# Diagonal 32x32 score blocks of the recurrent pairs made in the projection phase, and inverted on GpSimd in the recurrent phase straight from memory

## The chip, the cores and the metric
One core of a Trainium2 chip runs the whole kernel. The metric is the device time of one execution in microseconds. Engines: TensorE (PE, its weight loads PEld), VectorE (DVE), ScalarE (ACT), GpSimd (POOL) and SyncE (SP), which here issues nearly all DMAs, in program order on one queue.

## The reference, cut to what matters
Two layers over 1024 latent and 256 context tokens, batch 1. The change touches the RWKV-7 half of layer 0: eight heads of 64, forward and backward.

```python
def rwkv7_scan(r, w, k, v, a, bvec, state):
    xs = tuple(jnp.moveaxis(t.astype(jnp.float32), 2, 0) for t in (r, w, k, v, a, bvec))

    def step(s, inp):
        r_t, w_t, k_t, v_t, a_t, b_t = inp
        sa = jnp.einsum('bhvk,bhk->bhv', s, a_t)
        s = s * w_t[:, :, None, :] + sa[..., None] * b_t[:, :, None, :] + v_t[..., None] * k_t[:, :, None, :]
        return s, jnp.einsum('bhvk,bhk->bhv', s, r_t)
...
        return (rh, to_heads(w, RWKV_HEADS), kh, vh, -kk, kk * ah), bonus
```

The kernel does this scan in chunks of 128 tokens. The term with `sa` makes each chunk need the inverse of a triangular 128x128 matrix, the unit matrix less the strict triangle of the scores of `b` against `a`. The inverse is built from the inverses of its four diagonal 32x32 blocks.

## The kernel before, in words
All data are float32; large products are made from a high and a low part in three products. The phases run one after the other, with a barrier of all engines between them.

**Projection phase** (`project_phase`, L668). The input projection is made in 26 tiles of 128 columns (`TILES0`), each over 1280 tokens in three pieces (512, 512, 256). SyncE loads the weights two tiles ahead (L707). ScalarE evicts a tile (L911), VectorE shifts and mixes it (L479, L487), SyncE stores it (L796). Between these tiles the four pairs of heads are prepared: pair p has the five tiles from b = 5 + 5p. The table `PREP_PE` says behind which piece of which tile TensorE makes the small products of a pair, all in two PSUM banks, 6 and 7, in turn: `w0` and `a0` in tile b, `w1`, `a1` and `ksum` in tile b+1, `bonus` in tile b+5. A product waits until the last but one use of the banks is evicted. `w0` and `a0` read `wab` (`w_pair_lr`), which SyncE loads for the pair at tile b (L763). VectorE prepares the pair in steps at the head of its tiles (`prep`): step 3 ends with L995, step 4 with L1010, and step 0 of the next pair waits for `bonus` (L967). The results go to `in_d` (`put`, L751).

**Recurrent phase** (`rwkv_units`, L1044). Each pair is cut in two halves of five chunks: eight halves n. TensorE makes the scores of the five chunks (`bx`, `kx`, L1199), transposes (`nat`), `z`; then come `y32`, `d32`, `t32`, `y64`, `t64`, which build the 128x128 inverses, and `wu` and `out`, which use them. The scores of half n+1 stand ahead of the use of half n, and `y32(n)` stands at the last chunk of the scores of half n+1. The inversion goes round by memory: SyncE waits for the scores of half n in `N`, stores their diagonal blocks to `blk_d` in eight DMAs (L1110), and loads them again with one block to a partition, the forward ones to `U`, the backward ones to `Ut` (L1117). GpSimd turns the backward ones into `U` (L1561), and inverts by 30 steps of two instructions (L1566, L1568), then copies the transposes to `Ut` (L1573). SyncE stores both (L1126) and brings them back in 14 DMAs (L1122) to `XQ`, `XE` and `N`, for which `y32(n)` waits.

```python
                for n in range(HALVES):
                    if n + 1 < HALVES:
                        blocks_in(n + 1)
                    if n + 2 < HALVES:
                        for m in half_chunks(n + 2):
                            sp.wait_ge(s["out_dve"], m - NCH + 1)
                            load(m)
```

Of the kernel before, what the change touches and what calls it, by code (L numbers as in the profile page):

```python
# [55 lines left out]
def constants():  # L56
# [10 lines left out]
    c["side"] = ((p % 4) == np.arange(4)[None]).astype(one)  # L67
    c["neg"] = np.concatenate([np.where(f >= p, 0, -BIG), np.where(f <= p, 0, -BIG)], 1).astype(one)
    c["pick"] = np.concatenate([np.broadcast_to(p % 32 == 0, (P, P)), np.broadcast_to(p % 32 == 1, (P, P))], 1).astype(one)
# [7 lines left out]

    c["score"] = np.concatenate([(f > p), (f >= p), (f < p), (f <= p)], 1).astype(one)
    c["heads"] = ((p // 64) == (f // 64)).astype(one)
# [4 lines left out]
def const_layout():  # L84

    at, n = {}, 0
    for k, v in constants().items():
        at[k] = (n, n + v.shape[1])
        n += v.shape[1]
    return at, [at["parted16"][0], at["score"][0], n]  # L90
# [430 lines left out]
PREP_SEQ = [(name, p, i) for key in sorted(PREP_PE) for name, p in PREP_PE[key] for i in range(3)]  # L521
BY_ACT = [x for x in PREP_SEQ if x[0][0] in "wa"]
BY_DVE = [x for x in PREP_SEQ if x[0][0] not in "wa"]

# [143 lines left out]
def project_phase(nc, A, G, xnat, hi, lo, LW, LA):  # L668

    win = A.p["e_w_in"][0].rearrange("(k p) n -> p k n", p=P)  # L670
    with ExitStack() as ctx:
# [19 lines left out]
        mus, keep = sb("mix_mus", [P, 18, 4]), sb("mix_keep", [P, 18])  # L691
        PS = G.PS
# [20 lines left out]
        def job(n):  # L713
# [6 lines left out]
                "pp_ps by_act by_dve sq_ok c_ok ln_ok root e_ok pl_ok ready0 ready1 rk_ok kh_ok st0 st1 st_pl st_bonus pstep half_ok")  # L720
        with phase(nc, sems) as (block, s):
# [26 lines left out]
            def _(sp):  # L748
# [37 lines left out]
                sp.dma_start(G.cst_rwkv[:], A.consts[:, G.ends[1]:G.ends[2]]).then_inc(s["consts"], 16)  # L786
                for n in range(last + 1):
# [16 lines left out]
                sp.wait_ge(s["st_bonus"], 64)  # L804

            @block.tensor
            def _(pe):
                def prep_product(name, p):
                    for i in range(3):
                        x, bank = piece_of(name, p, i)  # L810
                        t, m = pieces(i)
                        if x >= 2:
# [2509 lines left out]
```

## Time and profile before

| | us |
|---|---|
| median of 3 runs | 3097.58 |
| lowest, highest | 3096.53, 3099.73 |
| the profiled execution | 3096.0 |
| its span in the trace | 3094.2 |
| TensorE busy | 2581.2 (83%) |
| VectorE busy | 1597.5 (52%) |
| ScalarE busy | 902.9 (29%) |
| GpSimd busy | 742.2 (24%) |

Times in the trace count from the span's start. The projection's tiles run from about 230 to 633 us and the recurrent phase from 640 to about 1165 us. The busy shares are means over many phases; what a change in one phase is worth has to be read there. PE slices in tenths, 40 of equal length: `6899999965688864676775999999599999998887`.

### The profile page before, as it was taken

Reading aid. Unit: us, or ns where it says so; the run is one execution under the profiler, and the core shown is the slowest. Engines: PE = TensorE matmul, PEld = TensorE weight load, DVE = VectorE, ACT = ScalarE, POOL = GpSimd, SP = SyncE. Lnnn points to the kernel's source line nnn. Section 1 sums busy time; section 2 is a strip of 40 time slices with the busy share of each in tenths; the row PEclk is TensorE's granted clock in tenths of the full one; section 3 lists DMA queues with packets and bytes.
Section 4 is the critical chain, followed back from the end, with each engine's and each line's share of the span. In section 5 each row is a group of like instructions: output and inputs, shape, how many; then the busy total and the mean of one; then the engine's idle time right before and its main releaser. Section 6 shows DMA issues by size and latency. Waiting matters only on the chain. (4 is left out here: it accounts for less than half of the span.)

```text
span 3094.2 us, 54814 instructions
## 1 busy us (share of the span) xinstructions
PE 2581.2 (83%) x23550; PEld 2185.8 (71%) x23550; DVE 1597.5 (52%) x2411; ACT 902.9 (29%) x1464; POOL 742.2 (24%) x739
## 2 busy tenths in 40 slices
PE   6899999965688864676775999999599999998887
PEld 2577677755677752555564777777499999998665
DVE  3037887542345624785466556465544646454233
ACT  2114333311132222563202232222233333332211
POOL 1111111126466541111322111111021111111421
PEclk8999999986889876677887999999799999999898
DMA  6622555532334413120461333232402222210621
GB/s 263 223 65 80 165 146 159 165 129 77 84 77 121 108 24 98 36 60 26 155 133 55 112 102 111 97 109 99 176 35 76 89 76 90 76 55 5 217 94 60
DMA packets 291551, 319.51 MB, mean 103 GB/s; under 512 B 109807, under 2 KB 235190, under 8 KB 288750
## 3 DMA queue, kind: packets, MB, share of 16 engines
q1 hardware_dynamic: 290240, 312.64, 32.1%
q8 instruction: 186, 3.05, 0.4%
q10 hardware_dynamic: 1070, 3.37, 0.3%
q14 instruction: 55, 0.45, 0.0%
HBM read 203.32 MB, written 112.56 MB: 102 GB/s over the span
## 5 line engine op out<-in xcount | busy, mean ns | idle before, releaser
L2895 PE MATMUL PS<-Q,K 128*128 128x128 f32 x2560 | 296.5, 278 | 31.1 <-DMA K<-k_d 23.6
L2895 PEld LDWEIGHTS PS<-Q,K 128*128 128x128 f32 x2560 | 293.0, 194 | 33.7 <-issue 27.6
L3016 POOL TENSOR_TENSOR weights_lo<-weights,weights_hi 128x1664 fp32r<-128x1664 f32 x32 | 121.3, 3791 | 566.3 <-ACT weights_hi L2974 566.3
L2922 PE MATMUL PS<-V_hi,weights_hi 128*128 128x258 f32 x832 | 239.1, 287 | 5.4 <-DVE H L3125 2.8
L461 PE MATMUL PS<-hT_hi,w_in_hi 128*128 128x512 f32 (+1 forms) x640 | 239.4, 374 | 0.0
L462 PE MATMUL PS<-hT_lo,w_in_hi 128*128 128x512 f32 (+1 forms) x640 | 236.3, 369 | 0.0
L2923 PE MATMUL PS<-V_lo,weights_hi 128*128 128x258 f32 x832 | 236.1, 284 | 0.0
L463 PE MATMUL PS<-hT_hi,w_in_lo 128*128 128x512 f32 (+1 forms) x640 | 236.0, 369 | 0.0
L2924 PE MATMUL PS<-V_hi,weights_lo 128*128 128x258 f32 x832 | 235.1, 283 | 0.0
L461 PE MATMUL PS<-h_hi,w_in_hi 128*128 128x512 f32 (+1 forms) x624 | 227.9, 365 | 5.3 <-PEq L112 5.3
L2396 PE MATMUL PS<-w_out_hi,y_in_hi 128*128 128x512 f32 x416 | 168.5, 405 | 71.6 <-POOL y_in_lo L2334 30.9
L462 PE MATMUL PS<-h_lo,w_in_hi 128*128 128x512 f32 (+1 forms) x624 | 224.5, 360 | 0.0
L463 PE MATMUL PS<-h_hi,w_in_lo 128*128 128x512 f32 (+1 forms) x624 | 223.9, 359 | 0.0
L2963 ACT ACTIVATE weights<-M_row,head_cols 128x128 f32<-128x128 f32 x352 | 112.2, 390 | 201.0 <-DVE diag_arg L3073 200.9
L2736 DVE SCALAR_TENSOR_TENSOR xnew<-padl,tile_cols,xnew 128x1024 f32<-128x1024 f32 x128 | 168.6, 1318 | 3.4
L2397 PE MATMUL PS<-w_out_lo,y_in_hi 128*128 128x512 f32 x416 | 167.0, 401 | 0.0
L2398 PE MATMUL PS<-w_out_hi,y_in_lo 128*128 128x512 f32 x416 | 166.6, 400 | 0.0
L2530 POOL TENSOR_TENSOR w_in_lo<-xnew,w_in_hi 128x2048 fp32r<-128x2048 f32 x15 | 69.3, 4618 | 404.1 <-ACT w_in_hi L2527 404.1
L925 POOL TENSOR_TENSOR w_in_lo<-w_in,w_in_hi 128x1024 fp32r<-128x1024 f32 x25 | 65.6, 2625 | 402.6 <-ACT w_in_hi L856 402.6
L2922 PEld LDWEIGHTS PS<-V_hi,weights_hi 128*128 128x128 f32 x832 | 157.9, 190 | 6.0 <-issue 6.0
L2923 PEld LDWEIGHTS PS<-V_lo,weights_hi 128*128 128x128 f32 x832 | 158.7, 191 | 0.0
L2924 PEld LDWEIGHTS PS<-V_hi,weights_lo 128*128 128x128 f32 x832 | 158.4, 190 | 0.0
(412 smaller groups left out, 5692.6 us busy)
## 6 DMA issues: line engine op xcount, KB each, us to landing
chunk_in<-in_d SPq DMA_DIRECT2D x40, 512.0 KB, 3.4
w_in<-in_e_w_in_dram SPq DMA_DIRECT2D x30, 512.0 KB, 5.1
xnew<-in_o_w_in_dram SPq DMA_DIRECT2D x30, 512.0 KB, 6.1
in_d<-xnat SPq DMA_DIRECT2D x20, 640.0 KB, 6.0
modw<-in_mod_w_dram SPq DMA_DIRECT2D x12, 1024.0 KB, 9.7
xnat<-in_mod_w_dram SPq DMA_DIRECT2D x8, 1536.0 KB, 7.4
v_d<-xnew SPq DMA_DIRECT2D x16, 640.0 KB, 3.0
k_d<-xc SPq DMA_DIRECT2D x16, 640.0 KB, 2.9
```

The lines of the kernel that those rows point to most:

```text
L461: pe.matmul(PS[:, bank + off // 512, 0:n], wh[:, k], hh[:, k, t], start=(k == 0), stop=False)
L462: pe.matmul(PS[:, bank + off // 512, 0:n], wh[:, k], hl[:, k, t], start=False, stop=False)
L463: last = pe.matmul(PS[:, bank + off // 512, 0:n], wl[:, k], hh[:, k, t], start=False, stop=(k == KT - 1))
L2396: pe.matmul(out, yh[:, i % YRING, t], wh[:, k, c], start=(k == 0), stop=False)
L2397: pe.matmul(out, yh[:, i % YRING, t], wl[:, k, c], start=False, stop=False)
L2398: last = pe.matmul(out, yl[:, i % YRING, t], wh[:, k, c], start=False, stop=(k == n_k - 1))
L2736: ins = dve.scalar_tensor_tensor(lat, padl[:, a:a + ROWS, b:b + GRID_W], col[tap], lat, ALU.mult, ALU.add)
L2895: last = pe.matmul(PS[:, 4 + x % 4, (j - j0) * P:(j - j0 + 1) * P], K[:, kt, j * P:(j + 1) * P], Q[:, kt, i * P:(i + 1) * P], start=(kt == ...
L2922: pe.matmul(out, wh, VH[:, j, q], start=(j == seen[0]), stop=False)
L2923: pe.matmul(out, wh, VL[:, j, q], start=False, stop=False)
L2924: last = pe.matmul(out, wl, VH[:, j, q], start=False, stop=(j == seen[-1]))
L3016: pool.tensor_tensor(WL[n % 2][:], W[:, n % 2], WH[n % 2][:].bitcast(F32), ALU.subtract).then_inc(s["w_lo"], 1)
```

## The change
The projection phase makes the diagonal blocks itself. Behind piece 1 of tile b+4 TensorE makes `blk0` (forward), behind piece 1 of tile b+5 `blk1` (backward, already transposed), each as 80 products of 64 rows and 32 columns in two bank uses. VectorE multiplies them by a triangle into `blk`: `blk0` at the end of step 4, `blk1` at the head of step 0. SyncE stores them to `blk_d` (`blocks_away`, eight DMAs each): those of `blk0` at tile b+5 ahead of the next pair's `wab`, those of `blk1` at tile b+6, the last ones ahead of the last tile's store.

In the recurrent phase the eight stores of a half, and GpSimd's first copy, are gone; both directions are loaded to `U`. The load for half n+1 stands right behind the store of the inverses of half n, and the 14 returns are a step of their own (`blocks_back`), which now waits for the scores in `N`. Constants are ordered anew: the pair's in the projection phase, the scores' at the head of the recurrent phase, `neg` and `block4` in the output phase.

```diff
+    c["tri"] = (np.arange(32)[None] > p % 32).astype(one)
...
-    PREP_PE[_b, 0], PREP_PE[_b, 1] = [("w0", _p)], [("a0", _p)]
+    PREP_PE[_b, 0], PREP_PE[_b, 1] = [("w0", _p)], [("a0", _p)] + ([("blk1", _p - 1)] if _p else [])
...
+    PREP_PE[_b + 4, 1] = [("blk0", _p)]
+PREP_PE[PREP_AT + 4 * PREP_TILES, 1] = [("blk1", 3)]
...
+                def blocks_away(p, d):
+
+                    sp.wait_ge(s["by_dve"], BY_DVE.index((f"blk{d}", p, 1)) + 1)
+                    for i in range(2):
+                        for k in range(4):
+                            sp.dma_start(A.blk_d[2 * p + i, d, 10 * k:10 * k + 10].rearrange("b s t -> s b t"),
+                                         blk[32 * k:32 * k + 32, 5 * i:5 * i + 5].rearrange("s c h t -> s (c h) t")).then_inc(s["blk_st"], 16)
+
                 def prep_io(n):
                     p, k = job(n)
                     if p is None:
                         return
+                    if k < 2 and p:
+                        blocks_away(p - 1, k)
                     if k == 0:
...
+                blocks_away(3, 1)
                 made(sp, last)
...
+                def block_product(p, d):
+
+                    ops = (aa[0], sg[0]) if d == 0 else (sg[1], kk)
+                    for h in range(2):
+                        x, bank = piece_of(f"blk{d}", p, h)
+                        bank_free(x)
+                        q = slice(64 * h, 64 * h + 64)
+                        for c in range(NCH):
+                            for k in range(4):
+                                t = slice(c * CH + 32 * k, c * CH + 32 * k + 32)
+                                ins = pe.matmul(PS[32 * k:32 * k + 32, bank, 32 * c:32 * c + 32], ops[0][q, t], ops[1][q, t],
+                                                start=True, stop=True)
+                        ins.then_inc(s["pp_ps"], 1)
...
+                            if name == "blk0":
+                                pe.wait_ge(ready[0], 4 * p + 3)
+                                block_product(p, 0)
+                            elif name == "blk1":
+                                pe.wait_ge(ready[1], 4 * p + 2)
+                                block_product(p, 1)
...
+                def blocks(p, d):
+                    if p or d:
+                        dve.wait_ge(s["blk_st"], 128 * (2 * p + d))
+                    for h in range(2):
+                        x, bank = piece_of(f"blk{d}", p, h)
+                        dve.wait_ge(s["pp_ps"], x + 1)
+                        dve.tensor_tensor(blk[:, :, h], PS[:, bank, 0:32 * NCH].rearrange("p (c t) -> p c t", t=32),
+                                          G.c("tri")[:, None, :].broadcast_to([P, NCH, 32]), ALU.mult).then_inc(s["by_dve"], 1)
...
                     if k == 0 and p:
+                        blocks(p - 1, 1)
                         dve.wait_ge(s["v_in"], 16 * p)
...
                         dve.scalar_tensor_tensor(khs, R, col(p, J_RK), khs, ALU.mult, ALU.mult).then_inc(s["rk_ok"], 1)
+                        blocks(p, 0)
...
                 def blocks_in(n):
-                    sp.wait_ge(s["bx_sb"], HC * (n + 1))
+
+                    if n:
+                        sp.wait_ge(s["zt_ok"], n)
+                        sp.wait_ge(s["zu_st"], 32 * n)
+                    else:
+                        sp.wait_ge(s["zero"], 1)
                     for d in range(2):
-                        for k in range(4):
-                            sp.dma_start(A.blk_d[n, d, 10 * k:10 * k + 10].rearrange("b s t -> s b t"),
-                                         diag(d, n, k, k).rearrange("s c h t -> s (c h) t")).then_inc(s["rel_st"], 16)
-                    sp.wait_ge(s["rel_st"], 128 * (n + 1))
-                    if n:
-                        sp.wait_ge(s["zu_st"], 32 * n)
-                        sp.wait_ge(s["zt_st"], 32 * n)
-                    for d, dst in enumerate((U, Ut)):
-                        sp.dma_start(dst[64 * d:64 * d + 40].rearrange("b s t -> b (s t)"),
+                        sp.dma_start(U[64 * d:64 * d + 40].rearrange("b s t -> b (s t)"),
                                      A.blk_d[n, d].rearrange("b s t -> b (s t)")).then_inc(s["rel_in"], 16)
...
+                sp.dma_start(G.cst_rwkv[:], A.consts[:, G.ends[3]:G.ends[4]]).then_inc(s["consts"], 16)
                 for m in half_chunks(0):
                     load(m)
+                blocks_in(0)
...
-                sp.wait_ge(s["zero"], 4)
-                blocks_in(0)
                 blocks_out(0)
+                blocks_in(1)
+                blocks_back(0)
...
-                    if n + 1 < HALVES:
-                        blocks_in(n + 1)
...
                         blocks_out(n + 1)
+                        if n + 2 < HALVES:
+                            blocks_in(n + 2)
+                        blocks_back(n + 1)
...
-                    step.link(pool.tensor_copy(U[64:104], Ut[64:104].rearrange("b s t -> b t s")))
+                    if n:
+                        pool.wait_ge(s["zt_st"], 32 * n)
```

SyncE at tile 10 of the projection, the first tile of pair 1, where `w_in` is a tile's weight load. Before:

```order
L796 DMA v_d<-p_out 128x1280 [waits mixed]
L707 DMA w_in<-in_e_w_in_dram 128x8x128 [waits lo_ok,hi_ok]
L763 DMA w_pair_lr<-in_rwkv_ww_f_dram 64x128 [waits pp_ps]
L763 DMA w_pair_lr<-in_rwkv_wa_f_dram 64x128
L763 DMA w_pair_lr<-in_rwkv_ww_b_dram 64x128
L763 DMA w_pair_lr<-in_rwkv_wa_b_dram 64x128
L766 DMA pair_bufs<-v_d 128x1280 [waits kh_ok]
```

The same place in the changed kernel:

```order
L812 DMA v_d<-p_out 128x1280 [waits mixed]
L713 DMA w_in<-in_e_w_in_dram 128x8x128 [waits lo_ok,hi_ok]
L764 DMA blk_d<-blocks_out 32x10x32 [waits by_dve]
L764 DMA blk_d<-blocks_out 32x10x32 x7
L779 DMA w_pair_lr<-in_rwkv_ww_f_dram 64x128 [waits pp_ps]
L779 DMA w_pair_lr<-in_rwkv_wa_f_dram 64x128
L779 DMA w_pair_lr<-in_rwkv_ww_b_dram 64x128
L779 DMA w_pair_lr<-in_rwkv_wa_b_dram 64x128
L782 DMA pair_bufs<-v_d 128x1280 [waits kh_ok]
```

Eight stores that wait for VectorE now stand between the weight load and the four loads of `w_pair_lr`.

SyncE in the recurrent phase, from the last chunk load of one half on. Before:

```order
L1104 DMA chunk_in<-v_d 128x128
L1126 DMA inv_d<-blocks 40x1024 [waits inv_ok]
L1126 DMA inv_d<-blocks 40x1024
L1126 DMA invt_d<-blocks_t 40x1024 [waits zt_ok]
L1126 DMA invt_d<-blocks_t 40x1024
L1122 DMA inv_first<-inv_d 32x10x32 [waits zu_st,y64_ps]
...
L1122 DMA chunk_scores<-invt_d 32x10x32 x4
L1110 DMA blk_d<-chunk_scores 32x10x32 [waits bx_sb]
L1110 DMA blk_d<-chunk_scores 32x10x32 x7
L1117 DMA blocks<-blk_d 40x1024 [waits zt_st,zu_st,rel_st]
L1117 DMA blocks_t<-blk_d 40x1024
L1103 DMA chunk_in<-in_d 128x1024 [waits out_dve]
```

The same place in the changed kernel:

```order
L1159 DMA chunk_in<-v_d 128x128
L1175 DMA inv_d<-blocks 40x1024 [waits inv_ok]
L1175 DMA inv_d<-blocks 40x1024
L1175 DMA invt_d<-blocks_t 40x1024 [waits zt_ok]
L1175 DMA invt_d<-blocks_t 40x1024
L1169 DMA blocks<-blk_d 40x1024 [waits zu_st,zt_ok]
L1169 DMA blocks<-blk_d 40x1024
L1185 DMA inv_first<-inv_d 32x10x32 [waits zu_st,y64_ps,bx_sb]
...
L1185 DMA chunk_scores<-invt_d 32x10x32 x4
L1158 DMA chunk_in<-in_d 128x1024 [waits out_dve]
```

The load of the next half's blocks has moved ahead of the returns, and the stores between are gone.

## Rows read from the trace of the kernel before

**Rows 1.** The list of waits, whole span: engine, line, waited for, total, times, longest.

```profile
PE PS L1259 <- DMA chunk_scores<-invt_d: 88.5, 8, 39.0
```

**Rows 2.** TensorE's timeline: start, us, line, operation, in brackets idle time and its releaser.

```profile
724.79 0.26 PE L1259 MATMUL PS<-inv_first,chunk_scores 32*32 32x32 f32 x1 [39.03 <-DMA chunk_scores<-invt_d]
...
786.10 0.26 PE L1259 MATMUL PS<-inv_first,chunk_scores 32*32 32x32 f32 x1 [12.40 <-DMA chunk_scores<-invt_d]
...
1139.19 0.26 PE L1259 MATMUL PS<-inv_first,chunk_scores 32*32 32x32 f32 x1 [21.70 <-DMA chunk_scores<-invt_d]
```

**Rows 3.** GpSimd's timeline, the first inversion.

```profile
675.63 1.99 POOL L1561 COPY blocks<-blocks_t 40x1024 f32<-40x1024 f32 x1 [31.65 <-DMA blocks_t<-blk_d]
677.68 0.16 POOL L1562 MEMSET blocks<- 104x32 f32 x1
...
713.04 1.91 POOL L1573 COPY blocks_t<-blocks 104x1024 f32<-104x1024 f32 x1
```

**Rows 4.** SyncE's timeline of DMA issues in the recurrent phase.

```profile
646.05 0.44 SPq L1104 DMA_DIRECT2D chunk_in<-v_d  x1
...
665.18 3.87 SPq L1110 DMA_DIRECT2D blk_d<-chunk_scores  x8
671.77 0.34 SPq L1117 DMA_DIRECT2D blocks<-blk_d  x1
...
713.01 0.65 SPq L1126 DMA_DIRECT2D inv_d<-blocks  x2
...
757.20 0.32 SPq L1103 DMA_DIRECT2D chunk_in<-in_d  x1
...
784.68 5.25 SPq L1110 DMA_DIRECT2D blk_d<-chunk_scores  x8
...
1058.20 1.35 SPq L1150 DMA_DIRECT2D sG_in<-g_d  x1
```

**Rows 5.** TensorE's timeline, small products and what follows them.

```profile
726.01 1.11 PE L1226 MATMUL PS<-cst,chunk_in 128*128 128x128 f32 x4
...
743.68 0.28 PE L1345 MATMUL PS<-chunk_in,wu 128*64 128x64 f32 x4
743.79 0.29 PE L1348 MATMUL PS<-wu,chunk_in 128*64 128x64 f32 x4
...
852.60 2.08 PE L1298 MATMUL PS<-inv_first,chunk_scores 64*64 64x64 f32 x34 [0.39 <-DVE inv_first L1610]
```

**Rows 6.** VectorE's timeline in the projection phase, and ScalarE's eviction of tile 9.

```profile
318.44 3.69 DVE L993 SCALAR_TENSOR_TENSOR xnat<-pair_bufs,xnat 128x1280 f32<-128x1280 f32 x1
344.01 1.55 DVE L1010 SCALAR_TENSOR_TENSOR pair_bufs<-pair_bufs,vc 128x1280 f32<-128x1280 f32 x1
...
440.91 1.55 DVE L1010 SCALAR_TENSOR_TENSOR pair_bufs<-pair_bufs,vc 128x1280 f32<-128x1280 f32 x1
...
530.12 1.55 DVE L1010 SCALAR_TENSOR_TENSOR pair_bufs<-pair_bufs,vc 128x1280 f32<-128x1280 f32 x1
...
328.67 1.24 ACT L911 ACTIVATE xnat<-PS 128x1280 f32<-128x1280 f32 x1 [11.59 <-PE PS L463]
```

**Rows 7.** SyncE's timeline, first and last of the four loads of pair 1.

```profile
331.37 1.16 SPq L763 DMA_DIRECT2D w_pair_lr<-in_rwkv_ww_f_dram  x1
...
333.86 0.60 SPq L763 DMA_DIRECT2D w_pair_lr<-in_rwkv_wa_b_dram  x1
```

**Rows 8.** TensorE's timeline, `w0` of pairs 1, 2 and 3.

```profile
336.86 3.67 PE L821 MATMUL PS<-LW,w_pair_lr 64*128 64x512 f32 x4 [2.77 <-DMA w_pair_lr<-in_rwkv_wa_b_dram]
...
435.93 3.75 PE L821 MATMUL PS<-LW,w_pair_lr 64*128 64x512 f32 x4 [5.02 <-DMA w_pair_lr<-in_rwkv_wa_b_dram]
...
530.95 3.21 PE L821 MATMUL PS<-LW,w_pair_lr 64*128 64x512 f32 x4 [3.80 <-DMA w_pair_lr<-in_rwkv_wa_b_dram]
```

**Rows 9.** Groups of instructions by line, 350 to 1100 us: count, busy us, mean ns, idle before.

```profile
L1604 DVE COPY chunk_in<-PS 128x256 f32<-128x256 f32 x40 | 16.8, 420 | 98.1 <-PE PS L1239 98.1
```

**Rows 10.** Busy us by stretch: PE, PEld, DVE, ACT, POOL; then PEclk, DMA share, GB/s.

```profile
337.00:347.00 10.00, 9.59 (x18) 5.27 (x19) 9.82 (x9) 3.02 (x4) 0.00 (x0) 0.50 0.66 183
```

More of the change, by code:

```diff
@@ L89, in const_layout @@
         n += v.shape[1]
-    return at, [at["parted16"][0], at["score"][0], n]
+    return at, [at["neg"][0], at["parted16"][0], at["heads"][0], at["score"][0], n]
 class Names:
@@ L804, in _, with bank_free @@
                 sp.wait_ge(s["st_bonus"], 64)
+                sp.wait_ge(s["blk_st"], 16 * 16 * 4)
             @block.tensor
             def _(pe):
+                def bank_free(x):
+                    if x >= 2:
+                        before = PREP_SEQ[x - 2]
+                        if before in BY_ACT:
+                            pe.wait_ge(s["by_act"], BY_ACT.index(before) + 1)
+                        else:
+                            pe.wait_ge(s["by_dve"], BY_DVE.index(before) + 1)
+                def block_product(p, d):
[10 more added lines that the diff above has]
+                        ins.then_inc(s["pp_ps"], 1)
                 def prep_product(name, p):
@@ L971, in prep @@
                             dve.wait_ge(st[1], 64 * p)
+                            dve.wait_ge(s["pp_ps"], PREP_SEQ.index(("blk1", p - 1, 1)) + 1)
                             dve.wait_ge(s["st_bonus"], 16 * p)
@@ L1055, in rwkv_units @@
         AR = [sb(f"key_scores{i}", [P, 2, 2, 2, P]) for i in range(2)]
+        G.cst_rwkv = sb("cst_rwkv", [P, G.ends[4] - G.ends[3]])
         U, Ut, tmp = sb("blocks", [P, 32, 32]), sb("blocks_t", [P, 32, 32]), sb("block_tmp", [P, 256])
@@ L1067, in rwkv_units @@
         loads = " ".join(f"ld{c}" for c in range(NCH))
-        sems = (loads + " once zero bx_ps bx_sb kx_ps kx_sb rk_sb nat_ps nat_sb z_ps z_sb rel_st rel_in inv_ok zt_ok zu_st zt_st x_in y32_ps y32_sb "
+        sems = (loads + " consts once zero bx_ps bx_sb kx_ps kx_sb rk_sb nat_ps nat_sb z_ps z_sb rel_in inv_ok zt_ok zu_st zt_st x_in y32_ps y32_sb "
                 "d32_ps d32_sb t32_ps t32_sb y64_ps y64_sb t64_ps t64_dve t64_act wu_ps wu_sb out_ps out_dve out_act "
@@ L1132, in blocks_out, with blocks_back, back @@
                     away(Ut, A.invt_d, s["zt_st"])
+                def blocks_back(n):
+                    def back(dst, src, k):
+                        sp.dma_start(dst, src[10 * k:10 * k + 10].rearrange("b s t -> s b t")).then_inc(s["x_in"], 16)
+                    sp.wait_ge(s["bx_sb"], HC * (n + 1))
                     if n:
                         sp.wait_ge(s["y64_ps"], n)
+                    else:
+                        sp.wait_ge(s["zero"], 4)
                     sp.wait_ge(s["zu_st"], 32 * (n + 1))
@@ L3234, in const @@
             if b <= ends[1]:
-                return G.cst0[:, a - ends[0]:b - ends[0]]
-            return G.cst_rwkv[:, a - ends[1]:b - ends[1]]
+                return G.cst_late[:, a - ends[0]:b - ends[0]]
+            if b <= ends[2]:
+                return G.cst0[:, a - ends[1]:b - ends[1]]
+            if b <= ends[3]:
+                return G.cst_pair[:, a - ends[2]:b - ends[2]]
+            return G.cst_rwkv[:, a - ends[3]:b - ends[3]]
         G.c = const
@@ L3253, in build @@
             gla_units(nc, A, G)
+        B = Names()
+        G.cst_late = sb("cst_late", [P, G.ends[1] - G.ends[0]])
+        B.gates = sb("gates1", [P, LRT])
         with ExitStack() as c1:
@@ L3264, in maps_in @@
                         eng.dma_start(B.wg[:, :, a, j], A.p[n][0][a * INNER:(a + 1) * INNER].rearrange("(t p) h -> p t h", p=P)).then_inc(sem, 16)
-                return 16
+                eng.dma_start(G.cst_late[:], A.consts[:, G.ends[0]:G.ends[1]]).then_inc(sem, 16)
+                return 17
             xnew = c1.enter_context(nc.sbuf_tensor("xnew", [P, NCH, D], F32))
```

33 lines of the change are left out of this document (14 added, 19 removed).

## The prediction
> **What bounds the kernel now.** I read four views in this order. The page's first table and its slices say that TensorE is busy 83% of the span, and that its busy share is down to 0.4 to 0.8 in slices 9 to 16, where the recurrent phase of the RWKV pairs lies. The list of waits then names what TensorE waits for there: the block inverses that come back from memory [rows 1]. 88.5 us of matmul idle time stand there, in eight waits, one for each half pair. The PE timeline shows the size of single ones [rows 2]: 39.03 us before the first `y32` product, 12.40 before the second, 21.70 before the last. The other 15.4 us are five short waits between. The other rows tell why. GpSimd starts the first inversion at 675.63 [rows 3], when SyncE has stored the blocks (L1110 from 665.18) and loaded them again (L1117 from 671.77) [rows 4], and both follow the scores of the half. From the last GpSimd product of an inversion to `y32` it takes 724.79 - 713.01 = 11.8 us [rows 2, 4]. So one half costs GpSimd a copy, 35.4 us of products [rows 3], and then the round trip. The way from the end of one inversion to the start of the next goes through two trips to memory, and TensorE waits for it.
>
> **Recurrent phase, what goes.** The eight block stores leave this phase, and the load for half n+1 stands right behind the store of the inverses of half n. GpSimd's period becomes 35.4 + 0.2 + 2.0 (the copy to `blocks_t`) + some 5 for store and load, about 43 us. TensorE's ready points for the first two waits are 685.8 and 773.7, and its stage from 724.79 to 773.7 takes 48.9 us. So GpSimd is no longer the bound.
> First half: SyncE issues the load of `blocks` after the last load of half 0 [rows 4], at 646.05 + 0.44, plus 0.45 for the constants that now stand ahead: 646.9. Issue to GpSimd's start took 675.63 - 671.77 = 3.9 us on a quiet queue; behind 2.9 MB of chunk loads I add 2.2 (my estimate, from 0 to 5): 653.0. Memset and products end at 688.6. With 11.8 for the way back and 0.7 for the next load, now ahead of it, `y32` starts at 701.1. TensorE is ready at 685.8 + 0.9, the 0.9 being the constants' load in front. So 14.4 of the 39.03 us stay.
> Halves 1 to 6: the return now starts when the chunk loads of the next half are issued, since the inverse is ready by then. Last load at 757.20 + 0.8, then 11.8 us less the copy of 2.0 plus the load of 0.7: 10.5, so 768.5 against a ready point of 773.7 [rows 2, 4]. 5 us of cover are left; if the loads in flight take it, the wait is back.
> Last half: the extra loads end at 1059.55; store of the inverses and load of the next blocks take 6.4, inversion 35.6, return 11.8: 1113.4 against a ready point of 1117.5. Covered by 4 us.
> Sum: 88.5 - 14.4 - 0.9 = **73.2 us saved**. TensorE's clock adds a little: in the stage after a wait it is at half speed. After the large waits at 786 and before 1139 some of that goes; I take 3 us (bounds 0 and 15). **-76 us.**
>
> **Projection phase, what comes.** Each pair gets two products of 80 matmuls of 64 rows and 32 columns, four evictions on VectorE, and 16 stores.
> *Matmuls.* No such shape is in the trace. The nearest is `y32`, whose 40 matmuls of 32x32 took 726.01 - 724.79 = 1.22 us at half clock, 30 ns each. In `out`, two products of 64 columns in two column halves of the same rows start 0.11 us before the next pair, 55 ns each. The upper bound is `y64`: 34 records, two to a matmul, in 2.08 us, 122 ns [rows 5]. I take 30 ns, the row of the same width: 2.4 us for 80 (bounds 1.6 and 9.8). The Trainium skill (TensorE: Matmul & The Clock Gate, Part 3) says that weight loads overlap running matmuls only where the row group differs; here four matmuls in turn share it. By that rule the 80 would run one by one; the two column halves in [rows 5] speak against it. Of eight products, `blk1` of all four pairs and the last `blk0` lie on TensorE's path: 5 x 2.4 = **12 us**. `blk0` of pairs 0 to 2 is hidden in the stall that comes next. It waits for VectorE's L993, done at 322.1 in pair 0 [rows 6], and TensorE reaches it when the last piece of tile 9 is due, some 3 us before that tile's eviction at 328.67 [rows 6], so it adds no wait of its own.
> *The new wait.* This is the term that matters. VectorE masks `blk0` at the end of its step 4, behind L1010. TensorE is one tile ahead of it: it wants `w0` of the next pair after piece 0 of the next tile. Two things now tie `w0` to VectorE. Its bank is the one that `blk0` used. And SyncE waits for the masked blocks, issues eight stores, and only then loads `w_pair_lr`, which `w0` reads. Before, that load was issued from 331.37 to 334.46 and `w0` ran at 336.86 [rows 7, 8]. Now: L1010 ends at 345.56 [rows 6]; two evictions of 320 columns at 0.53 each (scaled from 0.42 for 256 columns [rows 9]): 346.6; eight stores at 4.6 (3.87 and 5.25 were seen [rows 4]): 351.2; four loads 3.1, landing 2.4: 356.7. That is 19.9 us after 336.86. The same 11.2 us after L1010 give 453.6 against 435.93, 17.7 us, and 542.9 against 530.95, 12.0 us. These add up, since VectorE's work from tile b+2 to L1010 is one unbroken row that starts from an eviction of TensorE's tile: **49.6 us**. The clock costs nothing more: TensorE fell to 0.50 of full clock (1.2 GHz) after its 2.77 us of idle already [rows 8, 10].
> *End of the phase.* The last eight stores stand ahead of the last tile's store: **4.6 us**. The other evictions, 0.5 us each, lie in VectorE's wait for `bonus`. The stores of `blk1` lie in SyncE's idle time in the next tile.
> Together **+66 us**.
>
> **Rest.** The front load is 0.2 MB smaller, the same bytes come back in the output phase as a seventeenth load beside others: 0.
> Sum: -76 + 66 = **-10 us**. The profiled execution took 3096.0 us, so 3086; it lies 1.6 below the median of the three runs, which is inside their spread. A difference of 0.2% (6 us) is about what a measurement here can tell.
>
> **Rivals.**
> 1. *Slower: the returns queue behind chunk loads.* In halves 1 to 6 the 14 returns and the load of blocks are now issued within a microsecond of 2.9 MB of loads. For it: in [rows 4] they used to run alone. Against: 5 us of cover, and odd stages are longer. It decides from a delay of 5 us; at 10 us each, six halves give 30 back: 3116. Chance 0.13.
> 2. *Slower: the block products run one by one*, 9.8 us each, 5 x 7.4 = 37 more: 3123. For it, the rule named above and `y64`'s row; against, the column halves in `out`. By the skill's rule the time would come out here. Chance 0.12.
> 3. *The clock comes back with the waits.* If the use stages after the second, fourth, sixth and last half ran at full clock throughout, some 5 us each are won, 20 in all: 3066. For it, the half clock after waits; against, those stages have short waits of their own. Chance 0.13.
> 4. *The new wait is not there*, because `w0` is served from elsewhere or VectorE is earlier than in [rows 6]: 3036. I see no way in the code. Chance 0.04.
> The forecast itself has 0.58.
>
> **How the numbers follow.** 3086 with +-12 for the forecast's own bounds: stores at 3.87 or 5.25 move it by 3, the matmul pace between 20 and 55 ns by 10, the first half's load by 3. The range reaches to rival 3 below and to 3120 above, so that most of rival 1 is in and most of rival 2 out: 3060 to 3120. Faster by over 0.2%: 0.36 of the forecast's 0.58, and rivals 3 and 4: 0.53. Within 0.2%: 0.17 of the forecast and 0.02 of rival 1: 0.19. Slower: the rest, 0.28.
>
> **What would show it.** In the profile after: `y32` waits once, some 14 us, at the first half, and hardly after; GpSimd's first inversion starts some 22 us earlier in its phase than at 675.63, and each next one runs while TensorE uses the half before. In the projection phase TensorE's waits for `w_pair_lr` grow from 2.8, 5.0 and 3.8 us to about 23, 23 and 16. The first `y32` start lies some 42 us later than 724.79, since 66 us have come and 24 have gone by then. It is wrong if the three `w0` waits stay under 10 us, if a block product takes over 4 us, or if `y32` waits in the middle halves.

## The result, and the profile after

| | before | changed |
|---|---|---|
| median, us | 3098.55 | 3078.57 |
| lowest, highest, us | 3096.53, 3099.73 | 3075.57, 3090.57 |
| runs | 4 | 4 |
| the profiled execution, us | 3096.0 | 3090.57 |
| its mean granted clock | 0.899 | 0.904 |

The ratio is 0.9943, with a 95% interval from 0.9916 to 0.9971: faster by 9 to 26 us, best estimate 18. The forecast was 10 us, so the sign is right, and the time lies 7 us below the forecast and inside the range.

The two profiled executions differ by 5.4 us only, since the profile of the changed kernel is its slowest of four executions. All sums below are made between profiles, part by part; the 12 us between this profile and its median come back at the end. Among the executions of the experiments three fell out by far (3253.58, 6453.2 and 13092.65 us); medians and ratios leave these slow ones out.

First the list of waits of the changed kernel; L1319 answers to [rows 1]. Columns: engine, line waited at, releaser, total us, times, longest.

```profile
POOL blocks L1623 <- DMA blocks<-blk_d: 109.0, 8, 19.0
...
PE PS L856 <- DMA w_pair_lr<-in_rwkv_wa_b_dram: 44.8, 3, 19.7
...
PE PS L1319 <- DMA chunk_scores<-invt_d: 25.4, 4, 19.3
...
PE PS L844 <- issue: 5.6, 2, 3.2
...
PE PS L463 <- issue: 3.0, 2, 1.5
```

The wait for the block inverses fell from 88.5 us to 25.4. GpSimd still waits 109.0 us for blocks: it is now ahead of TensorE, and after the first half `y32` waits for inverses only 6.1 us in all. The wait of `w0` for `w_pair_lr` rose from 11.6 us, the sum of the three in [rows 8], to 44.8. Two lines are new and have no releaser at all: `issue`, on the block products (L844) and on the large product right behind them (L463), 8.6 us together.

TensorE's timeline, the `y32` products that waited; they answer to [rows 2]:

```profile
773.26 0.26 PE L1319 MATMUL PS<-inv_first,chunk_scores 32*32 32x32 f32 x1 [19.30 <-DMA chunk_scores<-invt_d]
...
821.92 0.21 PE L1319 MATMUL PS<-inv_first,chunk_scores 32*32 32x32 f32 x1 [1.14 <-DMA chunk_scores<-invt_d]
...
1092.87 0.21 PE L1319 MATMUL PS<-inv_first,chunk_scores 32*32 32x32 f32 x1 [1.53 <-DMA chunk_scores<-invt_d]
...
1133.32 0.26 PE L1319 MATMUL PS<-inv_first,chunk_scores 32*32 32x32 f32 x1 [3.41 <-DMA chunk_scores<-invt_d]
```

Only the first half still waits long. Where the phases begin and end is best read on SyncE: its first issue in the recurrent phase, and its first load of the phase after. Before the change:

```profile
640.52 0.32 SPq L1103 DMA_DIRECT2D chunk_in<-in_d  x1
...
1214.52 1.13 SPq L1795 DMA_DIRECT2D gla_nat<-gq_d  x2
```

and in the changed kernel, with the last stores of the projection phase and the load of the first blocks:

```profile
696.21 5.62 SPq L764 DMA_DIRECT2D blk_d<-blocks_out  x8
701.89 0.45 SPq L815 DMA_DIRECT2D gg_d<-p_out  x1
708.06 0.36 SPq L1220 DMA_DIRECT2D cst_rwkv<-in_consts_dram  x1
...
714.95 1.05 SPq L1169 DMA_DIRECT2D blocks<-blk_d  x2
...
1208.60 1.15 SPq L1857 DMA_DIRECT2D gla_nat<-gq_d  x2
```

The recurrent phase starts 708.06 - 640.52 = **67.5 us later**, and lasts 1208.60 - 708.06 = 500.5 us where it lasted 574.0, **73.5 us less**. What follows takes the same time (1879.7 and 1880.2 us to the end of the span). That is the whole account: +67.5 - 73.5 + 0.5.

**The 67.5 us.** TensorE's timeline at the first block product and the `w0` behind it:

```profile
328.20 1.53 PE L844 MATMUL PS<-xnat 64*32 64x32 f32 x154
...
332.96 0.33 PE L844 MATMUL PS<-xnat 64*32 64x32 f32 x6 [3.23 <-issue]
...
356.72 3.77 PE L856 MATMUL PS<-LW,w_pair_lr 64*128 64x512 f32 x4 [13.60 <-DMA w_pair_lr<-in_rwkv_wa_b_dram]
```

`w0` of pair 1 starts at 356.72 instead of 336.86 [rows 8], 19.9 us later. Those of pairs 2 and 3 follow:

```profile
475.53 3.78 PE L856 MATMUL PS<-LW,w_pair_lr 64*128 64x512 f32 x4 [19.75 <-DMA w_pair_lr<-in_rwkv_wa_b_dram]
...
581.95 3.78 PE L856 MATMUL PS<-LW,w_pair_lr 64*128 64x512 f32 x4 [11.50 <-DMA w_pair_lr<-in_rwkv_wa_b_dram]
```

against 435.93 and 530.95, so 39.6 and 51.0 us late. The chain behind it stands on VectorE and SyncE. VectorE:

```profile
346.55 1.55 DVE L1063 SCALAR_TENSOR_TENSOR pair_bufs<-pair_bufs,vc 128x1280 f32<-128x1280 f32 x1
348.01 0.88 DVE L1005 TENSOR_TENSOR blocks_out<-PS,cst_pair 128x320 f32<-128x320 f32 x2
```

SyncE:

```profile
348.92 3.86 SPq L764 DMA_DIRECT2D blk_d<-blocks_out  x8
352.83 0.47 SPq L779 DMA_DIRECT2D w_pair_lr<-in_rwkv_ww_f_dram  x1
...
354.62 0.60 SPq L779 DMA_DIRECT2D w_pair_lr<-in_rwkv_wa_b_dram  x1
```

The last preparation step ends, VectorE masks, SyncE stores eight times, and only then come the four loads that TensorE waits for. From L1063's end at 348.1 to `w0` it takes 8.6 us.

**The 73.5 us.** To the first `y32` it was 724.79 - 640.52 = 84.3 us and is 773.26 - 708.06 = 65.2: 19.1 less. Between the first and the last `y32` it was 414.4 us and is 360.1: 54.3 less. The rest is unchanged (75.3 and 75.3). Busy time in that middle stretch, before and after (columns: PE, PEld, DVE, ACT, POOL, then PEclk, DMA share, GB/s):

```profile
724.80:1139.20 414.40, 329.02 (x5699) 291.17 (x5699) 188.46 (x410) 103.72 (x232) 246.08 (x441) 0.85 0.34 88
```

```profile
773.30:1133.30 360.00, 320.03 (x5697) 284.09 (x5697) 181.62 (x410) 103.71 (x232) 227.78 (x423) 0.91 0.34 94
```

Of the 54.3 us, 43.4 are waits for inverses (88.5 - 39.0 = 49.5 before, 25.4 - 19.3 = 6.1 after). Of the other 10.9 us, 9.0 are TensorE's busy time (329.0 to 320.0): the same 5700 matmuls ran at a granted clock of 0.91 instead of 0.85. The last 1.9 are other idle time.

### The profile page after: what moved, and what is told of

The parts are those of the page before. It is cut to its first block and busy times, and to the rows that moved or that the text cites. A ratio compares the mean times of both kernels' runs of the same rounds, so it can differ in the third digit from the quotient of the medians.

```text
span 3088.8 us, 57409 instructions
## 1 busy us (share of the span) xinstructions
PE 2591.2 (84%) x24830; PEld 2195.6 (71%) x24830; DVE 1599.9 (52%) x2427; ACT 903.2 (29%) x1464; POOL 725.8 (23%) x731
## 5 line engine op out<-in xcount | busy, mean ns | idle before, releaser
L2957 PE MATMUL PS<-Q,K 128*128 128x128 f32 x2560 | 295.3, 277 | 32.5 <-DMA K<-k_d 24.1
L463 PE MATMUL PS<-hT_lo,w_in_hi 128*128 128x512 f32 (+1 forms) x640 | 236.8, 370 | 0.0
L463 PE MATMUL PS<-h_lo,w_in_hi 128*128 128x512 f32 (+1 forms) x624 | 227.6, 365 | 3.0 <-issue 3.0
```

The lines of the kernel that those rows point to most:

```text
L463: pe.matmul(PS[:, bank + off // 512, 0:n], wh[:, k], hl[:, k, t], start=False, stop=False)
L2957: last = pe.matmul(PS[:, 4 + x % 4, (j - j0) * P:(j - j0 + 1) * P], K[:, kt, j * P:(j + 1) * P], Q[:, kt, i * P:(i + 1) * P], start=(kt == ...
```

## The experiments

Each kernel was compared with the kernel before on the same chip: experiments 1 to 4 on one, 5 to 8 on a second, 9 and 10 on a third. The ratio of one kernel can differ by 0.0015 between chips (0.9790 and 0.9775 for the three edits), so small differences are read within a group. "Recurrent start" is the first issue of SyncE in that phase.

| run | median us | ratio to before, 95% | recurrent start | `w_pair_lr` wait | first `y32` wait |
|---|---|---|---|---|---|
| changed kernel again | 3079.16 | 0.9943 (0.9928 to 0.9958) | 704.31 | 44.2 | 18.4 |
| loads first | 3053.73 | 0.9868 (0.9853 to 0.9882) | 683.85 | 3.8, and 19.2 for a bank | 18.5 |
| mask early | 3046.54 | 0.9842 (0.9829 to 0.9856) | 675.53 | 15.3 | 18.7 |
| both | 3045.00 | 0.9829 (0.9814 to 0.9844) | 666.61 | 7.9 | 17.7 |
| both, block load first | 3031.19 | 0.9790 (0.9774 to 0.9806) | 665.52 | 7.7 | 6.8 |
| both, halves apart | 3037.04 | 0.9805 (0.9785 to 0.9825) | 658.97 | 7.6 | 18.8 |
| both, rows in turn | 3037.27 | 0.9808 (0.9789 to 0.9826) | 667.77 | 8.3 | 18.4 |
| projection part alone | 3161.30 | 1.0211 (1.0194 to 1.0228) | 703.88 | 44.5 | 38.4 |
| all four edits | 3022.46 | 0.9773 (0.9757 to 0.9788) | 659.64 | 7.8 | 6.9 |
| three edits again | 3027.16 | 0.9775 (0.9762 to 0.9789) | 665.5 | 8.0 | 8.0 |

**Theory.** The change pays in the recurrent phase what was forecast. It pays some 66 us for it in the projection phase, of which nearly 50 are one chain: mask behind step 4, stores, loads, `w0`. Nothing in what is computed asks for that order. Rival: the time in the projection phase is the price of the products and the evictions themselves.

### 1. Loads ahead of the stores

```diff
-                    if k < 2 and p:
+                    if k == 1 and p:
                         blocks_away(p - 1, k)
...
+                            blocks_away(p - 1, 0)
                             sp.wait_ge(s["kh_ok"], p)
```

SyncE issues the four `w_pair_lr` loads first, then stores `blk0`.

> The changed kernel, but at the first tile of a pair SyncE issues the four w_pair_lr loads first and the eight stores of blk0 behind them. Theory (w0 waits for the chain mask, stores, loads): w0 of pairs 1 to 3 is then held only by the bank that blk0 used, so it starts when VectorE has masked blk0, some 8 us earlier than the 356.7, 475.5 and 582.0 us of the changed kernel: 3 x 8 = 24 us off its median. Rival (the block products and their instruction traffic cost the time): the waits move, the time stays within 5 us.

The wait list shows the same wait under another name:

```profile
PE PS L857 <- DVE blocks_out L1006: 19.2, 3, 10.2
...
PEld PS L857 <- DMA w_pair_lr<-in_rwkv_wa_b_dram: 3.8, 1, 3.8
```

Where `w0` waited for its weights it now waits for the PSUM bank that the block product used, until VectorE has masked it (L1006). The phase ends 708.06 - 683.85 = 24.2 us earlier than in the changed kernel (20.5 earlier than in its repeat on the same chip, 704.31), and the time fell by 0.0075 of 3095, 23 us. The two ties of `w0` to VectorE are there, as the forecast said, one behind the other; the stores and loads were the later one.

### 2. Mask early

```diff
                     if k == 4:
+                        if p < 2:
+                            blocks(p, 0)
...
                         dve.wait_ge(ready[1], 4 * p + 2)
+                        if p == 2:
+                            blocks(p, 0)
...
-                        blocks(p, 0)
+                        if p == 3:
+                            blocks(p, 0)
```

VectorE masks `blk0` at the head of step 4 (pair 2: three operations in), not behind it.

> The changed kernel, but VectorE masks blk0 of pairs 0 and 1 at the head of step 4, of pair 2 three operations into it; pair 3 as before. Theory: stores and loads follow at once, so w0 starts at about 344, 466 and 573 in the changed kernel's times: 13 + 10 + 8, some 30 us off. Rival (block products): within 5 us.

```profile
PE PS L856 <- DMA w_pair_lr<-in_rwkv_wa_b_dram: 15.3, 3, 8.3
```

The wait for the weights fell from 44.8 us to 15.3, and the phase ends 32.5 us earlier (28.8 against the repeat). Time: 0.0101 less, 31 us. Six evictions of VectorE (two for each of three pairs) in another place are worth more than the whole change.

### 3. Both

Both diffs together.

> Both edits. Theory: w0 waits no longer than before the change (2.8, 5.0 and 3.8 us of idle time), 17 + 15 + 10 = 42 us off the changed kernel's median, to about 3037. If the two edits were independent costs their gains would add up to 54; the theory says they overlap, since each only shortens one chain. Rival: under 10 us.

```profile
PE PS L1325 <- DMA chunk_scores<-invt_d: 26.2, 3, 17.7
PE PS L1265 <- DMA chunk_in<-v_d: 19.0, 1, 19.0
PE PS L857 <- DMA w_pair_lr<-in_rwkv_wa_b_dram: 7.9, 2, 5.0
PE PS L845 <- issue: 5.0, 2, 3.0
```

The `w_pair_lr` wait is below that of the kernel before (11.6 us). The gain is 0.0114, 35 us, not the 42 expected: the phase starts 41.5 us earlier than in the profile of the changed kernel, but only 37.7 earlier than in the repeat below, which ran beside it. 23 and 31 don't add up to 54, because the two edits shorten the same chain. By the medians beside the repeat the three gains are 25, 33 and 34 us. What is left of the projection part is 666.61 - 640.52 = 26.1 us, for 8 block products, 16 evictions and 64 stores.

### 4. The changed kernel again

> The changed kernel unaltered, as the base for the others on the same chip. It should give 3078 +- 5; in its four runs it spread by 15 us (3075.57 to 3090.57), where the kernel before spread by 3, so I look for whether the spread comes back, and whether the waits for memory in the recurrent phase or the granted clock differ between executions.

The ratio came out the same, 0.9943, in an interval half as wide (the two medians alone, 3079.16 and 3095.14 us, give 0.9948). This profile starts the recurrent phase at 704.31, 3.8 us before the first one, with the same waits (44.2 us on `w_pair_lr`). So single profiles of this kernel differ by some 4 us in the projection phase alone. The recurrent phase takes 500.7 us here. In the profiles of experiments 1 and 2 (same chip), which leave this phase as it is, it takes 486.3 and 486.6, with the same waits for inverses and chunk loads (44.3 and 45.4 us for 45.3 here). What differs is TensorE's busy time, 387.6 and 386.4 us for 400.3, at a granted clock of 0.90 for 0.87. Experiment 3, with the same phase, has 495.7. So one profile of the recurrent phase is uncertain by some 14 us.

### 5. The first block load ahead of the chunk loads

```diff
+                blocks_in(0)
                 for m in half_chunks(0):
                     load(m)
-                blocks_in(0)
```

> Both earlier edits (loads first, mask early) kept; in the recurrent phase the first load of blocks stands ahead of the chunk loads of half 0. Theory: of the 19 us that the first y32 still waited, the part beyond the forecast's 14.4 is the 8.8 us that the block load needed from issue to GpSimd's start behind 2.9 MB of chunk loads. Ahead of them it should land in about 4, and it is issued some 5 us earlier, so GpSimd starts about 10 us earlier, the first y32 wait falls from 17.7 to about 8, minus under 1 us for the chunk loads that start later: 3045 - 9 = about 3036. Rival: the phase begins with a barrier, and GpSimd's memsets, not the load, set its first start: then the wait stays at 17 and the time at 3045. Second rival: the chunk loads start later by what the block load waits for, and the wait for chunk_in grows by as much as y32's falls: no gain.

GpSimd's timeline at the first inversion, with both edits and then with this one added:

```profile
681.59 0.16 POOL L1629 MEMSET blocks<- 104x32 f32 x1 [11.53 <-DMA blocks<-blk_d]
```

```profile
671.66 0.15 POOL L1629 MEMSET blocks<- 104x32 f32 x1 [2.69 <-DMA blocks<-blk_d]
```

It starts 6.1 us after the phase's start instead of 15.0. The first `y32` wait falls from 17.7 to 6.8 us and `chunk_in`'s grows from 19.0 to 20.7. Ratio: 0.0039 less than with both edits, 12 us, but on another chip; against `rows in turn` on the same chip, which has the same recurrent phase, it is 0.0018, 6 us, within the intervals. In the phase itself the first `y32` stands 54.8 us after the start for 63.5 (54.7 and 54.6 in experiments 10 and 9): 8.7 us earlier. The first rival (the memsets bound it) is out, the second holds for 1.7 us of 10.9. Behind ten chunk loads the load of 0.3 MB of blocks needed 8.8 us from its issue to GpSimd's start (714.95 to 723.75 in the changed kernel); the forecast had 3.9 + 2.2.

### 6. Block products in two halves

```diff
-def project_split(pe, PS, bank, wh, wl, hh, hl, pieces, at=0):
+def project_split(pe, PS, bank, wh, wl, hh, hl, pieces, at=0, midway=()):
...
+            if k == 3:
+                for job in midway:
+                    job()
...
-                                block_product(p, 0)
+                                block_product(p, 0, 0)
+                                midway = [lambda p=p: block_product(p, 0, 1)]
```

(the same for `blk1`). Forty products stand behind piece 1, forty behind the first 12 products of piece 2.

> Both earlier edits kept; TensorE makes only the first 40 products of a block product behind piece 1, the second 40 behind the first 12 products of piece 2. Theory: the idle stretches of 1.5 to 3.2 us with no releaser behind or inside a block product come from 80 small products in one row, faster than TensorE is supplied with instructions; with 40 in a row the supply holds (y32 has 40 in a row and shows none). Then the issue waits on the line of the block products and on the large product right behind them (7.3 us in all in the run with both edits) go to under 1, worth about 5 us with the half clock that follows them: about 3040. Rival: the idle time is a fixed event (for example code that is loaded at that place in the program) and does not depend on how many stand in a row: then it moves but stays, 3045.

```profile
PE PS L848 <- issue: 3.4, 4, 1.4
```

The idle time without a releaser fell from 7.3 us (5.0 on the block products, 2.3 on the large product behind) to 3.4, not to under 1. The phase starts 7.6 us earlier than in "both". Against kernels on the same chip it is 665.52 - 658.97 = 6.6 us (experiment 5, gaps of 8.1 us in all, 4.7 more than here) and 5.9 us (experiment 10 against 9, 7.3 against 2.7 us of gaps). So 4.6 to 4.7 us are the gaps and 1.3 to 1.9 us are left; that these are the clock is likely and not shown. In the end time nothing of it is seen: 0.9805 here, 0.9808 for `rows in turn` on the same chip.

The theory of the supply is not borne out. These are the two halves of the first block product:

```profile
326.81 0.89 PE L848 MATMUL PS<-xnat 64*32 64x32 f32 x80
...
329.26 0.74 PE L848 MATMUL PS<-xnat 64*32 64x32 f32 x62
331.44 0.37 PE L848 MATMUL PS<-xnat 64*32 64x32 f32 x18 [1.44 <-issue]
```

With the 12 large products between them the gap stands behind 80 + 12 + 62 = 154 records (two to a small product, one to a large one), and in the changed kernel it stands behind 154 too (328.20, x154). It is so at all four gaps: behind 154, 164, 130 and 167 records, counted from the start of the block product, in both kernels, and the other four block products have none in either. The gap ends 4.8 us after the start of the first block product in the changed kernel, 4.5 in "both" and 4.6 here (331.44 - 326.81). So the gap has a fixed place in the program, as the rival said. It got shorter because TensorE had 12 large products to do before it. How many small products stand in a row doesn't decide where it is. What happens at these places (the rival's example was code that is loaded) is in no record.

The clock in the same 12 us, first with the block product in one piece ("both"), then in two:

```profile
328.00:340.00 12.00, 9.00 (x197) 8.34 (x198) 11.69 (x12) 2.19 (x2) 0.47 (x1) 0.86 0.61 171
```

```profile
328.00:340.00 12.00, 10.29 (x130) 8.36 (x129) 11.69 (x12) 2.19 (x2) 3.46 (x1) 1.00 0.54 147
```

With the gap of 3.0 us the granted clock is 0.86 as a mean of this stretch, and so it is with the 3.2 us of experiment 5 on the same chip; with one of 1.4 it stayed at 1.00. In the next 12 us it is 0.86 in "both" and in experiment 5 and 1.00 here, but 0.72 in experiment 9, whose gap was 1.3 us. So the shorter gap doesn't always keep what it gains.

### 7. The two heads in turn

```diff
-                    for h in range(2):
...
+                    for c in range(NCH):
+                        for k in range(4):
+                            t = slice(c * CH + 32 * k, c * CH + 32 * k + 32)
+                            for h in range(2):
+                                bank = piece_of(f"blk{d}", p, h)[1]
```

> Both earlier edits kept; the 80 products are the same, but the two heads (rows 0 to 63 and 64 to 127) come in turn, so that each product reads other rows than the one before it. If weight loads overlapped only where the rows differ, the changed kernel's order (40 products on one half of the rows, then 40 on the other) would be held back by it and this order would be faster than 20 ns a product. Theory: the row group does not limit here, 160 records take 1.55 to 1.60 us as before, and the time stays at 3045. Rival: the burst gets shorter by a third or more (and the supply gap longer by as much).

`blk1` of pair 0 with the heads in turn, and below it the same product with one head after the other:

```profile
356.46 1.55 PE L846 MATMUL PS<-pair_bufs,xnat 64*32 64x32 f32 x160 [0.66 <-ACT xnat L917]
```

```profile
356.56 1.57 PE L845 MATMUL PS<-pair_bufs,xnat 64*32 64x32 f32 x160 [0.25 <-ACT xnat L915]
```

80 products of two records each take 1.55 and 1.57 us: 19.4 and 19.6 ns a product, whether neighbours share their 64 rows or not. The rule of the Trainium skill (TensorE: Matmul & The Clock Gate, Part 3), that weight loads overlap only where the row group differs, doesn't show here in either direction: the trace disagrees with it. In each of the two orders, though, a product differs from the one before it in its 64 rows or in the group of 32 output rows; neighbours that share both were not tried. (The same section also lets a weight load run ahead when it goes to a background weight buffer, which I left out of the prediction; with that the trace agrees.) The time is that of "both" within what two jobs can tell.

### 8. The projection part alone

The projection phase of the changed kernel with the recurrent phase of before (its stores, its loads into `U` and `Ut`, GpSimd's copy), so that each block is made twice.

```diff
+                for n in range(HALVES):
+                    if n + 1 < HALVES:
+                        blocks_in(n + 1)
...
+                    step.link(pool.tensor_copy(U[64:104], Ut[64:104].rearrange("b s t -> b t s")))
```

> One part of the change alone: the projection phase of the changed kernel (block products, masks, stores, late w_pair_lr loads) with the recurrent phase of before, which makes, stores and loads its blocks itself and turns the backward ones on GpSimd. The stores of the projection phase are then of no use. Theory: the two parts of the change don't touch each other, so the recurrent phase starts at about 708 as in the changed kernel and takes the 574 us of before from its first issue to the first load of the next phase; the time is before + 68: about 3163. Rival: part of the time lost in the projection phase is given back by something at the phase's start (a drained queue, the clock), then it is under 3155.

3161.3 us against 3163 expected; its start at 703.88 is 63.4 after 640.52, and the time is 3161.3 - 3096.0 = 65.3 us above that of the kernel before on this chip. The wait list has the old wait back:

```profile
PE PS L1315 <- DMA chunk_scores<-invt_d: 88.0, 8, 38.4
PE PS L856 <- DMA w_pair_lr<-in_rwkv_wa_b_dram: 44.5, 3, 19.1
```

The parts don't touch each other. Between this kernel and the changed one the ratio falls from 1.0211 to 0.9943, by 0.0268: the recurrent part alone brings 83 us, by the ratios, where the pair of profiles gave 73.5 and the forecast 76. The difference between 83 and 73.5 is of the size by which profiles of this phase differ (experiment 4).

### 9 and 10. All four edits, and three again beside them

Diffs 1, 2, 5 and 6 together; and 1, 2 and 5.

> All four edits together: loads first, mask early, block load first, halves apart. Theory: the edit on the block load acts in the recurrent phase (first y32 wait 17.7 to 6.8) and the halves apart in the projection phase (recurrent phase begins 7.6 us earlier), so they add up: 3045 - 12 - 7 = about 3026, 70 us below the kernel before. The first y32 wait should stay near 7 and the recurrent phase should begin near 658. Rival: the block load first only helped because the projection phase ended where it did, or the halves apart gave the clock at the wrong place; then the time stays at that of the better single edit, about 3031 to 3034.

> The same kernel as in the run with the block load first, beside the one with all four edits on the same chip, so that the two can be compared. Theory: 3031, and some 5 to 7 us above the kernel with all four. Rival: no difference between the two beyond 2 us.

With all four: 3022.46 us, ratio 0.9773, **72 us below the kernel before** and, by the ratios (0.9943 and 0.9773), 53 below the changed one. The first `y32` wait is 6.9 and the recurrent phase starts 5.9 us before that of the three edits, so both effects are there. In the end times the medians differ by 4.7 us, but the ratios, 0.9773 and 0.9775 with intervals of 0.0015 to either side, can't tell the two apart. The first two edits are shown to help in the end time; so is the third, by 0.0039 and 0.0054 below "both" on other chips, though its size lies between 6 and 17 us; the fourth only within its phase.

## Why the prediction was right, point by point

**The new wait of `w0`: right, to the size.** `w0` of pair 1 was put at 356.7 and stands at 356.72. The three delays were to be 19.9, 17.7 and 12.0, together 49.6; the third `w0` is 51.0 us late. That the first came out to the hundredth is chance: the last step ended 2.5 us later than taken (348.1 for 345.56), and the way from there took 8.6 us for 11.2, with stores at 3.86 and loads that landed sooner. Experiments 1 and 2 show that both ties are real, and that the larger cause is where VectorE masks. The waits themselves were forecast at 23, 23 and 16 us and are 13.60, 19.75 and 11.50, because TensorE arrived later than I let it: 343.1 (356.72 - 13.60) instead of 334.1. This hides in the wait and costs nothing. In the terms of the sum it is why the cost of `blk0`'s products was rightly left out.

**The matmuls: right sum, wrong parts.** 2.4 us for 80 was taken (30 ns each), 1.57 was measured (20 ns). But 8.6 us of `issue` waits came with the eight products, and a lower clock behind the longest of them. Five products on the path at 1.57 are 8 us where I had 12. Three of the four gaps (1.50, 2.42 and 1.47 us) stand at products on the path, 5.4 us together; the longest, 3.23, is at `blk0` of pair 0 and lies ahead of the 13.60 us for which `w0` waits anyway. That makes 13 us for 12, without what the clock costs behind them. The sum came out because the gaps, which the forecast didn't have, fill what the pace left: that is luck.
The step that failed is the sentence "No such shape is in the trace". It was there, in the page of groups and in the waits of the phase after, in the kernel before:

```profile
L1920 PE MATMUL PS<-lev_x 64*32 64x32 f32 x3200 | 35.5, 211 | 39.8 <-issue 28.0 <-DVE gla_blocks L2207 9.3 <-ACT gla_A L2058 2.5
```

35.5 us for 1600 products are 22 ns each, and `issue` stands beside them with 28.0 us in 12 waits. That one row had both the pace and the gap. The rival of one-by-one products it could not have settled, since its neighbours read the two halves of the rows in turn (`rows(d)`, L1920); experiment 7 does.

**End of the phase: right.** Eight stores at 5.62 us, 4.6 forecast. Together +66 forecast, +67.5 and +63.8 in two profiles, +63.4 in experiment 8.

**First half of the recurrent phase: right mechanism, too small a price.** 14.4 us of wait were to stay, 19.3 stayed. The term that was mis-sized is the load of `blocks` behind the chunk loads: 3.9 + 2.2 taken, 8.8 measured. I had given it a range up to 5 us on top of 3.9; the measured 4.9 sits at its end. GpSimd starts 15.7 us after the phase's start instead of 35.1, 19 earlier where 22 were forecast. The first `y32` lies 48.5 us later than before, 42 forecast; of the 6.2 us between the two (701.1 + 66 - 724.79 = 42.3 forecast), 2.7 are this load, 0.5 its later issue, 1.4 the inversion and the way back, and 1.5 the later start of the phase.

**Halves 1 to 6: right, with rival 1 at its threshold.** The forecast gave the returns 10.5 us after the last chunk load and 5 us of cover. At the second half:

```profile
804.98 0.43 SPq L1159 DMA_DIRECT2D chunk_in<-v_d  x1
805.46 0.73 SPq L1175 DMA_DIRECT2D inv_d<-blocks  x2
806.23 2.90 SPq L1175 DMA_DIRECT2D invt_d<-blocks_t  x2
811.79 0.65 SPq L1169 DMA_DIRECT2D blocks<-blk_d  x2
```

and `y32` at 821.92, 16.5 us after 805.41. The delay behind the chunk loads is 6.0 us, and 1.14 of it shows as a wait. Rival 1 asked for a delay above 5 to decide; it is there, but four of the six halves have no wait at all, so it costs 2.7 us in all instead of 30.

**Last half: nearly right.** Put at no wait with 4 us of cover; 3.41 are left.

**The clock: mechanism right, size too small.** 3 us were taken, with a bound of 15; the middle stretch gave 9.0 in busy time (0.85 to 0.91) and 1.9 in other idle time. Rival 3 had asked for 20. In the profiles the waits that stayed beyond the forecast (4.9 + 6.1) and what the middle stretch gave beyond it (10.9 - 3) cancel but for 3 us, so 73.5 stands against 76. That they nearly cancel is luck.

**The total.** The profile says -5.4, the medians -20, the ratio -18. The account of waits is that of the profile; the other executions left none. The profiled execution is 12 us above its kernel's median at a mean clock of 0.904; the others have 0.907 to 0.909. If all of the time went with the clock, 0.004 of 3089 us would be 12 us (an estimate). So what the forecast missed in the total goes with the granted clock again. One place where the same code gains that much is known from experiments 1 and 2: the recurrent phase, 14 us shorter at 0.90 for 0.87. With the 9 to 11 us above that is the 20 of rival 3 and more, so the clock can give what that rival priced, and the forecast's 3 us for it was the term that was too small. What makes one execution keep more of the clock than another stays open.

## What to carry to other kernels

Work moved off a critical wait into an earlier phase costs less by its own duration (here 13 us of products) than by what stands behind it in the queues, so follow each moved instruction on its engine down to the next load that waits behind it, and ask whether it has to stand ahead: here two such reorderings gave 35 us back. Look for the shape of a new instruction in all of the trace, the phases included that the change doesn't touch, before it is priced from a neighbour. The first item of a pipelined stage deserves its own look: its small load belongs ahead of bulk loads that nobody wants sooner.

## What the runs showed of the hardware that was not expected

- TensorE stands without instructions for 1.5 to 3.2 us in or right behind four of eight rows of 80 small products (160 records of 64x32, 20 ns a product), with no releaser. The gaps stand behind the same number of TensorE's records in the changed kernel and with the rows in two halves, whether 12 large products stand before them or not; the first gap ended 4.4 to 4.8 us after the start of its row, and work moved ahead of it filled part of it (1.4 us left of 3.0).
- Behind a gap of 3 us in a stretch of steady large products the granted clock was 0.86 over 12 us, and 1.00 with the shorter gap. Over the whole phase 4.6 to 4.7 us less of gaps went with a start that was 5.9 to 6.6 us earlier, on the same chip.
- The same recurrent phase took 500.5 and 500.7 us in two profiles and 486.3 and 486.6 in two others, with the same waits: the granted clock was 0.87 in the first two and 0.90 in the others.
- The load of blocks took 8.8 us from issue to use behind ten chunk loads, and with an empty queue ahead 4.8 (666.84 to 671.66 in experiment 5), though it is the same load.
- Between 230 and 325 us all kernels run the same large products nearly without a break. The granted clock there was 1.00 in the profile of before, 0.98 in those of the changed kernel and of experiments 1 to 4, and 1.00 in those of 5 to 10. Experiment 8 has the projection phase of the changed kernel, so it isn't the program that makes the difference.
